# Three groups of steps at other places in a hand-written order: head 0's scores and weighing, two sets of shift products, the inverse's last step

## The chip, the core and the metric

The kernel runs on one core of a Trainium2 chip. Its engines each work through their own queue in the order in which the program issues to them: PE (TensorE, matmuls and transposes), DVE (VectorE), ACT (ScalarE), POOL (GpSimd, some additions and the feed of one weight stream) and SP (SyncE, the main weight stream). They meet only at semaphores. The metric is the device time of one launch in microseconds (us).

## The reference, cut to what matters

512 tokens of width 1024 go through a differential attention layer, then through a feed-forward layer, a mixer (pooling and a gated delta rule in chunks of 64) and a second feed-forward layer, each of the last three behind an RMS norm that is scaled and shifted by a conditioning vector. Everything is float32. Cut to the three places that the change touches:

```
# attention, 16 heads: two score maps a head, softmax each, weighed difference
a = softmax(q1 @ k1.T / 8 - slope * distance) - lam * softmax(q2 @ k2.T / 8 - slope * distance)
o = (1 - 0.2) * rms_norm(a @ v) * g

# each sublayer of the second block
h = rms_norm(x, norm_g) * (1 + scale) + shift          # then h @ w_in

# delta rule: one unit lower triangular system of 64 rows per head and chunk
sol = triangular_solve(a_mat + eye, rhs, lower=True, unit_diagonal=True)
```

## The kernel before, in words

`Plan` writes one list of steps by hand. Every engine walks the whole list and issues its own part of each step, in list order, so the place of a step in the list is its place in five queues at once. Nothing reorders them afterwards.

The unit of time in the list is one `mm` step: one 128x128 block of weights against 512 tokens, as three matmuls (lines 1202, 1203 and 1205) because the weights (`wH`, `wL`) and the activations (`hH`, `hL`) are kept as a high and a low part. The weights of 8 such blocks are a slot. SP loads a slot into `wr`, ACT writes its high part (line 1908, step `split`), DVE its low part (line 1497, same step). The `split` of slot j+3 stands behind the last block of slot j.

**Attention.** Iteration i of the loop over heads has 24 list positions, one behind each `mm` of the tiles q, k and v of head i (in iteration 1, q of head 1 has been done ahead, and positions 8 to 15 stand behind the blocks of k, 16 to 23 behind those of v). `SCHED` says at which position which small step of an earlier head stands; a position of 24 or more falls into the next iteration. Where several stand at one position, those from an earlier iteration come first, then `rstd`, `sq_lo`, `table`, `scores`, `weigh`, `turnw` and `ada`, in that order. For head 0 in iteration 1 `c0` and `w0` hold, for all others `c` and `w`.

- `scores` (query blocks of 128 rows): PE multiplies q by k (line 1266) into two of the banks 2, 3 and 4, DVE adds the distance term and takes the row maximum (line 1620, then line 1624), ACT exponentiates and sums (line 2007). Block 3 takes banks 3 and 4, and bank 4 is free when DVE has read block 2 in it.
- `weigh`: DVE alone, four dependent operations (lines 1630 to 1639), after the exponentials. It signals `w`.
- `turnw` (key block kb): PE transposes the weighed blocks kb to 3 (line 1278). For kb 0 the last transpose waits for `w` of block 3. The step of head 0 stands at position 4 of iteration 2.
- `rstd`: PE sums squares (line 1255), ACT takes Ln and Exp (lines 1996 and 1999), DVE scales q and k (line 1609). That of head 1 stands at position 1 of iteration 2.
- `ada`: PE products of the conditioning vector with weights that POOL feeds (line 1302).

**Shift products.** The first tiles behind a norm are multiplied by x before its norm is known. The shift's part of them is made apart: `shift_row` (lines 1543 and 1546, eight dependent DVE operations on a slot still in `wr`), and later `shift_sum` on PE (line 1219). Norm 1 has three such rows, during the output tiles of attention (16 blocks a tile, steps (c, k) = tile and block); norm 2 has two, during the output tiles of the first feed-forward layer (22 blocks a tile).

**Inverse.** `inverse(g, step)` for g 0 and 1 makes the five steps t, p5, y5, p6, y6, three ticks apart (a tick is one `mm` or one `pool_out` block). y6 (line 1426) multiplies on PE, and ACT and DVE copy its two banks back (lines 2156 and 1847).

Of the kernel before, what the change touches and what calls it, by code (L numbers as in the profile page):

```python
# [46 lines left out]
def shape_constants():  # L47
# [18 lines left out]
    for g, w in enumerate((2, 4, 8, 16)):  # L66
# [3 lines left out]
    return c  # L70

SCHED = {"rstd": 1, "v": 10, "table": 2, "c": [(9, (0, 1)), (14, (2,)), (18, (3,))], "w": [11, 12, 16, 21],
         "c0": [(14, (0, 1)), (17, (2,)), (20, (3,))], "w0": [16, 17, 19, 22], "d": [4, 7, 7, 13], "pv": 18, "ada": 30,
         "o": 5, "lo": (12, 18)}


# [34 lines left out]
def src(name, col, nk=8, row=0, cols=128):  # L111
    return (name, row, nk, col, cols)
# [19 lines left out]
class Plan:  # L132
# [13 lines left out]
    def sig(self, name):  # L146
        self.count[name] = self.count.get(name, 0) + 1
        return self.count[name]
# [4 lines left out]
    def add(self, what, **d):  # L153
        self.steps.append((what, d))
        return d
# [338 lines left out]
    def out0(self):  # L494
        sig, add = self.sig, self.add
        add("fold0", rn=self.count["rn"])
        z_free = [("gl", 0)] * 4
        zr = Ring(range(4))
        for h in range(6, HEADS):
            i, _ = zr.take()  # L500
            d = dict(h=h, i=i, free=z_free[i], zs=sig("zs"), zm=sig("zm"), gh=sig("gh"), gl=sig("gl"), on=self.on[h])
            z_free[i] = ("gl", d["gl"])
            self.whole(Tile("z", src("l0_w_in", 6144 + 128 * h), self.pb01.take()[1], "h", ("zs", d["zs"]), n=0, d=d))
            if h < 12:
                add("fold", h=h - 6, ze=h - 5, gh=sig("gh"), gl=sig("gl"))
        self.h_lasts[1] = len(self.slots)
        self.move("x_back", zm=self.count["zm"])
        self.move("mod_in")
        add("mod_wait")
        sq_free = [("gl", self.count["gl"])] * 4  # L510
        self.square_ring = zr

        def square(c):
            i, _ = zr.take()
            z_free[i] = self.square(1, c, v=("zb", i), free=z_free[i], acc_free=("gl", self.count["gl"]))

        first = len(self.slots) + 16
        more = {4: [lambda: add("mod_rest"), lambda: self.raw(1, 0), lambda: self.raw(1, 1)],
                5: [lambda c=c: self.raw(1, c) for c in (2, 3, 4)], 6: [lambda: self.raw(1, 5)], 7: [lambda: self.raw(1, 6)]}
        at = {(6, 9): lambda: self.shift_row(1, 0, first), (7, 1): lambda: self.shift_row(1, 1, first + 1),  # L520
              (7, 8): lambda: self.shift_row(1, 2, first + 2)}
        for c in range(8):
            r = sig("xr")
            t = Tile("res0", src("l0_w_out", 128 * c, 16), self.pb01.take()[1], "g", ("xr", r), c=c, xr=r)
            for k in self.steps_of(t):
                if k == 5 and c > 0:
                    square(c - 1)
                    for fn in more.get(c, []):
                        fn()
                if (c, k) in at:  # L530
                    at[c, k]()
            if c == 3:
                add("mod", modt=sig("modt"))
        self.last_square = lambda: square(7)

    def ffn(self, sub, w_in, w_out):
        sig, add = self.sig, self.add
        n = {0: 1, 2: 3}[sub]
        f = sub // 2
        add("ffn", f=f, n=n)  # L540
        pb = Ring(range(6))

        def gate(j, rhs="h"):
            fg = sig("fg")
            if rhs == "h":
                return Tile("gate", src(w_in, 128 * j), pb.take()[1], "h", ("fg", fg), n=n, j=j, f=f, fg=fg)
            gr = sig("gr")
            return Tile("gate", src(w_in, 128 * j), pb.take()[1], "r", ("gr", gr), n=n, j=j, f=f, fg=fg, gr=gr)

        def up(j, rhs="h"):  # L550
            d = dict(fu=sig("fu"), ah=sig("ah"), al=sig("al"))
            return Tile("up", src(w_in, FFN + 128 * j), pb.take()[1], rhs, ("fu", d["fu"]), n=n, j=j, f=f, fg=22 * f + j + 1,
                        **d)

        self.raw_start(n, gate(0, "r"), up(0, "r"), gate(1, "r"))
        self.whole(up(1))
        for j in range(2, 22):
            self.whole(gate(j))
            self.whole(up(j))
        self.h_lasts[n + 1] = len(self.slots)  # L560
        ring, s_free = Ring(range(2)), [("rs", 0)] * 2

        def square(c):
            i, _ = ring.take()
            s_free[i] = self.square(n + 1, c, v=("sq", f, i), free=s_free[i], acc_free=("nl", 8 * n + 8))

        first = len(self.slots) + 24
        for c in range(8):
            r = sig("xr")
            t = Tile("res", src(w_out, 128 * c, 22), pb.take()[1], "a", ("xr", r), c=c, xr=r, sub=sub, f=f, back=None)  # L570
            for k in self.steps_of(t):
                if k == 5 and c > 0:
                    square(c - 1)
                    if n == 1:
                        self.raw(2, c - 1)
                if n == 1 and c == 7 and k in (2, 9):
                    self.shift_row(2, k // 9, first + k // 9)
        self.last_square = lambda: square(7)
        if n == 3:
            square(7)  # L580

    def mixer(self):
        sig, add = self.sig, self.add
        n = 2
# [54 lines left out]
        def at(tick, fn, *a):  # L639

            n_ev[0] += 1
            events.append((tick, n_ev[0], fn, a))
# [138 lines left out]
        at(227, lambda: add("sol_back"))  # L781
        for g in range(2):
            for j, step in enumerate(("t", "p5", "y5", "p6", "y6")):
                at(251 + 16 * g + 3 * j, inverse, g, step)
        po = iter(range(8))
        for which in "kq":
            for g in range(2):
# [30 lines left out]
        for t in range(4):  # L818
            if t > 0:
                for g in range(2):  # L820
                    d = dict(g=g, t=t, ks=sig("ks"), rr=[sig("rr") for _ in range(4)], ur=ur[g], st=st[g])
# [14 lines left out]
            for g in range(2):  # L836
                om[g] = sig("om")
                d = dict(g=g, t=t, at=ro.take()[1], om=om[g], vv=vv[g], hq=sig("hq"), hn=sig("hn"), i=(2 * t + g) % 4)
# [37 lines left out]
        first = len(self.slots) + 8  # L876
# [1473 lines left out]
```

## Time and profile before

| | |
|---|---|
| median of 3 runs | 1902.35 us (1902.47, 1902.35, 1899.78) |
| profiled execution, its own time | 1900.43 us |
| its span, first to last instruction | 1898.6 us |
| mean granted TensorE clock | 0.997 |
| PE busy | 1869.9 us (98%) |
| DVE busy | 995.5 us (52%) |
| ACT busy | 818.2 us (43%) |
| POOL busy | 124.0 us (7%) |

Times inside a profile count from the start of its span. The profiled execution's own time is 1.83 us above the span, which is what lies ahead of the first and behind the last instruction. A row of a timeline gives the start, the length, the engine, the line and the operation, and in brackets how long the engine sat idle before it and what released it.

### The profile page before, as it was taken

To read this page: it belongs to the slowest core of one execution; us is meant where nothing else is said; L and a number is where in the kernel's file an instruction comes from. 1 tells how busy PE (TensorE), PEld (TensorE's weight loads), DVE (VectorE), ACT (ScalarE), POOL (GpSimd) and SP (SyncE) were. 2 spreads that over 40 slices of the span, in tenths; PEclk is the share of its full clock that TensorE was granted. 3 is DMA by queue.
4 is the path that set the end of the run, shared out by engine and by line. 5 is a ranking of instruction groups with operands and counts; after the bars stand their busy time and mean duration, and the time that the engine had idled before them with its cause. 6 is when DMAs were issued, how large, how long until landed. Compare 5 with 4: busy or idle time off the path is not lost.

```text
span 1898.6 us, 22387 instructions
## 1 busy us (share of the span) xinstructions
PE 1869.9 (98%) x8923; PEld 1448.7 (76%) x8923; DVE 995.5 (52%) x1778; ACT 818.2 (43%) x1328; POOL 124.0 (7%) x148
## 2 busy tenths in 40 slices
PE   8999999999999999999999999999999999999997
PEld 6566666666788788888886777778888878888886
DVE  6667666665544653333346667845434763333322
ACT  6566656656643342222324655434432442222221
POOL 0101111110001000000010011000000100000000
PEclk9999999999999999999999999999999999999999
DMA  5534333332233132222323313221123323222221
GB/s 199 182 127 162 137 144 145 146 143 101 78 132 114 67 111 100 95 95 93 100 87 124 104 65 106 70 92 35 45 89 111 124 90 103 94 100 97 92 93 62
DMA packets 56526, 201.95 MB, mean 106 GB/s; under 512 B 6478, under 2 KB 6934, under 8 KB 55784
## 3 DMA queue, kind: packets, MB, share of 16 engines
q1 hardware_dynamic: 44616, 158.32, 23.7%
q0 software_dynamic: 11808, 42.21, 6.1%
q8 instruction: 71, 1.16, 0.2%
q14 instruction: 31, 0.25, 0.0%
HBM read 195.23 MB, written 5.28 MB: 106 GB/s over the span
## 4 chain that ended last, share of the span: by engine, by line
PE 84%; DVE 8%; ACT 6%; issue 2%; DMA 0%; SPq 0%; DVEq 0%; ACTq 0%
PE ps L1202 24%; PE ps L1205 23%; PE ps L1203 23%; ACT wH L1908 2%; PE ps L1302 2%; PE ps L1338 1%; DVE a L1620 1%; DVE wL L1497 1%; PE ps L1266 1%; ACT a L2007 1%; PE ps L1290 1%; PE ps L1278 1%; PE ps L1345 1%; DVE g1a L1497 1%; PE ps L1255 1%
## 5 line engine op out<-in xcount | busy, mean ns | idle before, releaser
L1202 PE MATMUL ps<-hH,wH 128*128 128x512 f32 (+1 forms) x1560 | 635.7, 408 | 1.0 <-DVE hL L1568 1.0
L1205 PE MATMUL ps<-hH,wL 128*128 128x512 f32 (+1 forms) x1560 | 610.3, 391 | 1.0 <-DVE wL L1497 0.7
L1203 PE MATMUL ps<-hL,wH 128*128 128x512 f32 (+1 forms) x1560 | 608.7, 390 | 0.0
L1497 DVE TENSOR_TENSOR wL<-wr,wH 128x1024 fp32r<-128x1024 f32 (+2 forms) x285 | 343.9, 1207 | 490.8 <-ACT wH L1908 490.2
L1908 ACT ACTIVATE wH<-wr 128x1024 fp32r<-128x1024 f32 (+2 forms) x285 | 295.2, 1036 | 234.3 <-PE ps L1205 220.4
L1202 PEld LDWEIGHTS ps<-hH,wH 128*128 128x128 f32 (+1 forms) x1560 | 292.5, 187 | 97.0 <-issue 36.2
L1205 PEld LDWEIGHTS ps<-hH,wL 128*128 128x128 f32 (+1 forms) x1560 | 292.3, 187 | 67.5 <-DVE wL L1497 3.9
L1203 PEld LDWEIGHTS ps<-hL,wH 128*128 128x128 f32 (+1 forms) x1560 | 292.9, 188 | 60.7 <-issue 6.5
L1202 PE MATMUL ps<-gffn,wH 128*128 128x512 f32 x400 | 156.9, 392 | 1.0 <-DVE xT L1675 0.8
L1205 PE MATMUL ps<-gffn,wL 128*128 128x512 f32 x400 | 155.7, 389 | 0.0
L1203 PE MATMUL ps<-gffn,wH 128*128 128x512 f32 x400 | 155.6, 389 | 0.0
L2007 ACT ACTIVATE a<-a,tiny 128x128 f32<-128x128 f32 (+3 forms) x128 | 71.0, 555 | 154.3 <-DVE tiny L1624 154.3
L1908 ACT ACTIVATE gffn<-affn 128x512 fp32r<-128x512 f32 x44 | 27.8, 632 | 184.2 <-DVE affn L1697 181.0
L1202 PE MATMUL ps<-g,wH 128*128 128x512 f32 x224 | 89.1, 398 | 0.0
L1202 PEld LDWEIGHTS ps<-gffn,wH 128*128 128x128 f32 x400 | 75.1, 188 | 17.7 <-DVE xT L1675 1.3
L1203 PE MATMUL ps<-g,wH 128*128 128x512 f32 x224 | 87.4, 390 | 0.0
L1205 PE MATMUL ps<-g,wL 128*128 128x512 f32 x224 | 87.2, 389 | 0.0
L1203 PEld LDWEIGHTS ps<-gffn,wH 128*128 128x128 f32 x400 | 75.1, 188 | 15.8 <-issue 0.5
L1205 PEld LDWEIGHTS ps<-gffn,wL 128*128 128x128 f32 x400 | 75.1, 188 | 15.8
L1697 DVE TENSOR_TENSOR affn<-ps,affn 128x512 f32<-128x512 f32 x42 | 29.0, 691 | 101.9 <-PE ps L1205 100.1
L2062 ACT ACTIVATE affn<-ps 128x512 f32<-128x512 f32 x40 | 23.9, 597 | 117.0 <-PE ps L1205 117.0
L2234 POOL TENSOR_TENSOR affn<-affn 128x512 f32<-128x512 f32 x12 | 18.5, 1545 | 693.6 <-ACT affn L1934 693.6
(304 smaller groups left out, 2079.4 us busy)
## 6 DMA issues: line engine op xcount, KB each, us to landing
wr<-wst SPq DMA_DIRECT2D x268, 512.0 KB, 3.4
a<-wfd POOLq DMA_DIRECT2D x54, 512.0 KB, 4.8
xT<-wfd POOLq DMA_DIRECT2D x18, 512.0 KB, 6.8
wr<-wst SPq DMA_DIRECT2D x16, 384.0 KB, 2.9
xT<-xin SPq DMA_DIRECT2D x8, 256.0 KB, 7.5
xT<-xin SPq DMA_DIRECT2D x2, 1024.0 KB, 6.3
xsave<-xT SPq DMA_DIRECT2D x1, 2048.0 KB, 7.3
c<-wfd POOLq DMA_DIRECT2D x8, 256.0 KB, 3.4
```

Source lines behind the costliest of these rows:

```text
L1202: e.matmul(o, hi, xh[k], start=k == 0, stop=False)
L1203: e.matmul(o, hi, xl[k], start=False, stop=False)
L1205: i = e.matmul(o, lo, xh[k], start=False, stop=k == t.nk - 1)
L1255: e.matmul(b[:], m, sq_hi[j], start=True, stop=False)
L1266: i = e.matmul(ps[d["banks"][m]][:, a["at"]:a["at"] + n], qn[h % 2][64 * m:64 * m + 64, 128 * qb:128 * qb + 128], kn[h % 2][64 * m:64 * m ...
L1278: i = e.transpose(b4(b, qb - kb), Wr[h % 2][:, a:a + 128], C("ident"))
L1302: i = e.matmul(ps[7][32 * j:32 * j + 1, :], csil[:, k:k + 1], ada_buf[a % ADA_BUFS][:, 512 * (j % 2):512 * (j % 2) + 512], start=k == 0, s ...
L1497: e.tensor_tensor(dst, x, hi.bitcast(F32), ALU.subtract).then_inc(s[name], 1)
L1697: e.tensor_tensor(v, ps[t.bank][:], f["sg"][j % 2], ALU.mult).then_inc(s["fu"], 1)
L1908: e.activation(dst, x, ACT.Copy).then_inc(s[name], 1)
L2007: e.activation(v, v, ACT.Exp, bias=mx[:, m:m + 1], accum_out=rsum[:, m:m + 1]).then_inc(s["ex"], 1)
L2062: e.activation(v, ps[t.bank][:], ACT.Silu).then_inc(s["fg"], 1)
```

## The change

`scores` of head 0 go from positions 14, 17 and 20 (blocks 0 and 1, block 2, block 3) to 14, 20 and 23. Its `weigh` steps go from 16, 17, 19 and 22 to 17, 18, 22 and 26, and 26 is position 2 of iteration 2. The three shift rows of norm 1 go from (6, 9), (7, 1), (7, 8) to (5, 11), (6, 3), (6, 11), the two of norm 2 from (7, 2), (7, 9) to (6, 12), (7, 2). The y6 steps stand two ticks later, for g 0 and g 1. No instruction is added, taken away or altered in size.

```
-         "c0": [(14, (0, 1)), (17, (2,)), (20, (3,))], "w0": [16, 17, 19, 22], "d": [4, 7, 7, 13], "pv": 18, "ada": 30,
+         "c0": [(14, (0, 1)), (20, (2,)), (23, (3,))], "w0": [17, 18, 22, 26], "d": [4, 7, 7, 13], "pv": 18, "ada": 30,
...
-        at = {(6, 9): lambda: self.shift_row(1, 0, first), (7, 1): lambda: self.shift_row(1, 1, first + 1),
-              (7, 8): lambda: self.shift_row(1, 2, first + 2)}
+        at = {(5, 11): lambda: self.shift_row(1, 0, first), (6, 3): lambda: self.shift_row(1, 1, first + 1),
+              (6, 11): lambda: self.shift_row(1, 2, first + 2)}
...
-                if n == 1 and c == 7 and k in (2, 9):
-                    self.shift_row(2, k // 9, first + k // 9)
+                if n == 1 and (c, k) in ((6, 12), (7, 2)):
+                    self.shift_row(2, c - 6, first + c - 6)
...
-                at(251 + 16 * g + 3 * j, inverse, g, step)
+                at(251 + 16 * g + 3 * j + j // 4 * 2, inverse, g, step)
```

## Rows read from the trace of the kernel before

**Rows 1.** The profile's page, part 1: busy time of each engine.

```profile
PE 1869.9 (98%) x8923; PEld 1448.7 (76%) x8923; DVE 995.5 (52%) x1778; ACT 818.2 (43%) x1328; POOL 124.0 (7%) x148
```

**Rows 2.** Who PE waited for: us in total, times, longest.

```profile
PE ps L1266 <- DVE tiny L1620: 2.3, 1, 2.3
...
PE ps L1402 <- DVE a L1836: 1.5, 1, 1.5
```

**Rows 3.** Timeline of PE around head 0's scores: start, length, engine, line, idle before.

```profile
58.08 1.13 PE L1266 MATMUL ps<-a 64*128 64x512 f32 x4 [2.32 <-DVE tiny L1620]
...
67.72 0.60 PE L1278 MATMUL ps<-cst,a 128*128 128x128 f32 x4
68.07 0.48 PE L1202 MATMUL ps<-hH,wH 128*128 128x512 f32 x1
...
68.85 0.40 PE L1202 MATMUL ps<-hH,wH 128*128 128x512 f32 x1
...
69.54 0.39 PE L1202 MATMUL ps<-hH,wH 128*128 128x512 f32 x1
```

**Rows 4.** Timeline of DVE in the same stretch.

```profile
57.37 0.56 DVE L1620 CUSTOM_DVE_ANT_0 a<-ps,a 128x384 f32<-128x384 f32 x1
...
58.53 0.16 DVE L1630 RECIPROCAL tiny<-tiny 128x2 f32<-128x2 f32 x1
...
59.76 0.69 DVE L1497 TENSOR_TENSOR g1a<-a,g1a 128x512 fp32r<-128x512 f32 x1
60.36 0.16 DVE L1630 RECIPROCAL tiny<-tiny 128x2 f32<-128x2 f32 x1
...
61.80 0.69 DVE L1620 CUSTOM_DVE_ANT_0 a<-ps,a 128x512 f32<-128x512 f32 x1
...
64.90 0.17 DVE L1630 RECIPROCAL tiny<-tiny 128x2 f32<-128x2 f32 x1 [1.59 <-ACT a L2007]
...
66.54 0.69 DVE L1584 COPY xT<-ps 128x512 f32<-128x512 f32 x1
...
68.28 0.74 DVE L1609 SCALAR_TENSOR_TENSOR a<-a,tiny,xT 128x512 f32<-128x512 f32 x1
```

**Rows 5.** Timeline of ACT in the same stretch.

```profile
58.65 0.61 ACT L2007 ACTIVATE a<-a,tiny 128x384 f32<-128x384 f32 x1 [3.68 <-DVE tiny L1624]
...
59.77 0.19 ACT L2007 ACTIVATION_READ_ACCUMULATOR a<-a,tiny 128x1 f32 x1
63.34 0.72 ACT L2007 ACTIVATE a<-a,tiny 128x512 f32<-128x512 f32 x1 [3.38 <-DVE tiny L1624]
...
65.72 1.24 ACT L1996 ACTIVATE xT<-ps,cst 128x512 f32<-128x512 f32 x2
66.86 1.15 ACT L1999 ACTIVATE xT<-xT 128x512 f32<-128x512 f32 x2
```

**Rows 6.** A window: length; PE, PEld, DVE, ACT, POOL busy; granted clock; DMA.

```profile
1289.58:1292.99 3.41, 3.41 (x14) 2.37 (x13) 0.69 (x1) 0.69 (x2) 0.00 (x0) 0.50 0.02 5
```

**Rows 7.** Timeline of PE and DVE at the end of attention's output tiles.

```profile
641.24 2.68 DVE L1546 SCALAR_TENSOR_TENSOR b<-wr,tiny,b 128x128 f32<-128x128 f32 x7
...
643.34 0.39 PE L1205 MATMUL ps<-g,wL 128*128 128x512 f32 x1
...
643.83 0.69 DVE L1675 TENSOR_TENSOR xT<-ps,xT 128x512 f32<-128x512 f32 x1
```

**Rows 8.** The page, part 6: DMA issues, KB each, us to landing.

```profile
wr<-wst SPq DMA_DIRECT2D x268, 512.0 KB, 3.4
```

**Rows 9.** Timeline of DVE at the end of the first feed-forward layer.

```profile
1005.05 1.23 DVE L1497 TENSOR_TENSOR wL<-wr,wH 128x1024 fp32r<-128x1024 f32 x1 [1.30 <-ACT wH L1908]
```

**Rows 10.** Timeline of PE and ACT around y6 of g 0.

```profile
1273.88 2.08 PE L1426 MATMUL ps<-a 64*64 64x64 f32 x32
1275.06 0.59 ACT L2156 ACTIVATE a<-ps 64x512 f32<-64x512 f32 x1 [1.17 <-PE ps L1426]
...
1278.75 1.91 PE L1381 MATMUL ps<-cst,a 128*128 128x128 f32 x16
```

## The prediction

> **What bounds the kernel now.** The page comes first: PE is busy for 98% of the span, the next engine for 52% [rows 1]. No PE instruction is added or taken away, so all that the change can do is to open or close gaps in PE's work. The list of what PE waited for comes next. Of its waits two lie at steps that the change touches or stands beside: 2.3 us in one piece at line 1266, head 0's scores, and 1.5 us at line 1402, y5 of the inverse [rows 2]. So the most that the attention part can win is 2.3 us, 0.12% of the time, less than what a measurement of this kernel can tell from no change (0.2%, 3.8 us). What it can lose has no such limit, so I follow each queue around the new places.
>
> **Why PE waits at head 0's scores now.** PE reaches `scores` of block 3 at 58.08 - 2.32 = 55.76 and starts at 58.08 [rows 3]. It needs bank 4, in which block 2 stands until DVE has taken its maximum, and DVE starts on that at 57.37 [rows 4]: 0.71 from the start of DVE's instruction to PE. DVE was late for that, not PE.
>
> **The attention part, step by step.** The new order on DVE behind the `split` and `weigh` of block 0, which it finishes at 57.37 as before, since what is ahead of them stays, is: `sq_lo` of head 1's k, `weigh` 1, maxima of block 2, `weigh` 2, the copy of v, a `split`, maxima of block 3, `rstd` of head 1, `weigh` 3. The lengths are start to start from [rows 4]: block 2's maxima 58.53 - 57.37 = 1.16; `weigh` 1 59.76 - 58.53 = 1.23; `sq_lo` 0.60; `weigh` 2 61.80 - 60.36 = 1.44; `weigh` 3 66.54 - 64.90 = 1.64; copy and `split` together 68.28 - 66.54 = 1.74. Block 3's maxima start at 61.80 and ACT starts its exponentials at 63.34 [rows 4, 5]: 1.54, of which 1.34 is DVE's up to its last small operation.
>
> - DVE starts block 2's maxima at 57.37 + 0.60 + 1.23 = 59.20, ready at 60.36.
> - PE reaches `scores` of block 3 three `mm` steps later than before. A step is 69.54 - 68.85 = 0.69 [rows 3], so 55.76 + 2.07 = 57.83. It can start at 59.20 + 0.71 = 59.91. The wait of 2.32 becomes one of 2.08. That is all the gain, 0.24: two more pieces of DVE work now stand ahead of block 2, and PE is given about as much time as they take.
> - ACT exponentiates block 2 in 59.77 + 0.19 - 58.65 = 1.31, begun 0.12 after DVE is through (58.65 against 58.53) [rows 4, 5]: 60.48 to 61.79. `weigh` 2 waits for it (before, it was ready): 61.80 to 63.24. Copy and `split` to 64.98.
> - Block 3's maxima 64.98, exponentials from 66.52, done 64.90 - 63.34 = 1.56 later [rows 4, 5]: 68.08.
> - ACT only then turns to `rstd` of head 1: two Ln in 66.86 - 65.72 = 1.14, then the first Exp, half of 1.15 plus about 0.1 to reach DVE [rows 5]: 68.08 + 1.14 + 0.66 = 69.88. Its PE sums are long there: by PE's order they are done before `ada`, so well ahead of the 67.48 below.
> - DVE scales q and k of head 1, two operations of 0.74 that overlap to about 1.35 [rows 4]: 71.2. `weigh` 3 takes 1.64 and ends at about 72.85. Before it ended at 66.54, because it stood ahead of the copy, the `split` and `rstd`.
>
> PE gets to `turnw` of kb 0 at 67.72 in the kernel before, and goes on with the next `mm` at 68.07 [rows 3]. Now it gets there at 67.72 - 0.24 = 67.48. Three of its transposes can run; the fourth waits for `weigh` 3, and the next `mm` starts at about 73.1. **This part therefore costs 73.1 - 68.07 = 5.0 us**, as one stop of about 5.3 us less the 0.24. Everything behind the stopped transpose on PE waits with it: the remaining blocks of head 2's q, hence its `out_qk` on ACT and the next `split`. These hang on PE, so they arrive late by the same 5.0 and are not late against it. Nothing later takes it back, since PE is the busy engine and none of its later waits hangs on a clock of its own. POOL's `table` for head 1 waits for block 3's maxima (by the sum above 66.5 instead of 63.3), and the maxima of head 1, which read it, come more than 10 us later; the feed of `ada` behind it has the same cover. SP has no step that moves.
>
> The bounds of this part: if `rstd` came through on ACT before block 3 (it stands behind it in the list, so this needs my order to be wrong), the stop would be shorter by 1.8 + 1.35, about 2 us left. If DVE loses time where I overlap, up to 1 us more. Taken: 5.0, between 2 and 6.
>
> **The clock.** The stop has a second price that no instruction shows. The granted clock was 0.50 for 3.41 us from 1289.58 [rows 6], that is 1.2 instead of 2.4 GHz. It fell after PE had waited 1.5 us [rows 2] and then done narrow 32-row products, an estimate of 2.5 us with little work in all. It didn't fall after the 2.32 us at 58.08. A stop of 5.3 us is twice either. One stretch at half clock costs at most 3.41 / 2 = 1.7 us. I take 1.6, and 0 to 3.4 (none, or two stretches) as bounds. The Trainium skill, "TensorE: Matmul & The Clock Gate", section "HAM oscillation — how this bites in real kernels", says that a wait between bursts of matmuls sets PE back to half its clock and that the rise is paid again each time; it speaks against this change, and without it the sum would be 1.6 us lower. The trace agrees in kind with its 0.50 from 1289.58.
>
> **Shift rows of norm 1.** Each row is one operation and seven of 2.68 us together, some 3.0 us of DVE [rows 7]. The last one ended on 643.83, when DVE took up the sum for x; PE's last product there began at 643.34 and was over at 643.73 [rows 7]. So DVE was late by 0.1 us or less, and only that is won: 0.06. The rows go to a tile earlier, where DVE has the same room, behind the `split` of the same stretch, and the slot that each reads is there: SP asks for it once the `split` four slots earlier is done, which stands 12 `mm` steps ahead, 8.3 us, and a slot lands in 3.4 us [rows 8]. If it were late, DVE would wait, and behind it on DVE a `split` that PE needs some 9 us later: still 0. POOL adds squares beside the second one, which slows DVE there by about a microsecond, hidden by the same cover. Without that cover it would cost its 1 us.
>
> **Shift rows of norm 2.** DVE was waiting for ACT again, 1.30 us, before the last tile's last `split` [rows 9], so the old rows held nobody up. 0, between -0.1 and +0.3.
>
> **y6 two ticks later.** y6 of g 0 starts at 1273.88, ACT copies at 1275.06, and the next step that takes one of its banks starts at 1278.75 [rows 10]. Two `mm` steps are 1.4 us, so the copy ends at about 1277.0: still early. PE waited for neither y6, so nothing is won. The wait at y5 is DVE's copy behind a conv step, which stays. 0, between -0.3 and +0.3; without the gap of 3 us it would cost up to the 1.4.
>
> **The sum.** 5.0 + 1.6 - 0.06 = +6.6 us. Against the profiled execution's own 1900.43 that is 1907.0. The median of the runs shown is 1.9 higher, 1902.35, and would give 1908.9. The four executions at hand lie at 1899.78, 1900.43, 1902.35 and 1902.47, and I take their middle, 1901.4: **1908.0 us**.
>
> **The rivals.**
>
> - *The stop costs no clock, and the stretch at half clock at 1289.58 goes.* That one hangs on a short stop of 1.5 us, so a small shift might spare it; for it speaks that a similar stop at 58.08 cost no clock. Against it: the new stop is much longer. 5.0 - 1.6 = 3.4, on 1901.4: 1904.8, within 0.2% of before. 0.20.
> - *No new wait (other side: faster).* The place is the fourth transpose at 67.48. If `weigh` 3 is done by then, nothing is lost, and if the wait at the scores goes too, 2.3 is won: 1899.1. For it: DVE is busy for 52% only, so there is room. Against it: the chain from block 2's maxima on is dependent work on two engines, and needs 5.3 us less than its own rows give. It decides only where that chain shortens by all of 5.3. 0.04.
> - *The clock stays low for longer* or falls at both stops, 57.83 and 67.5: 5.0 + 3.4 and the stretch at 1289.58 kept: 1909.8, and with DVE's lost microsecond 1911. 0.12.
>
> **How the numbers follow.** The forecast has 0.64, with a range of its own from 1905.5 to 1911.0: 1901.4 or 1902.35 as base, 4 to 6 for the stop, 0 to 3.4 for the clock. The range for all is 1903.5 to 1911.5. It takes in the first rival and most of the last, and leaves out the one on the other side and the tails. Slower by over 0.2% (above 1906.15) are the forecast and the last rival less their low ends: 0.73. Within 0.2%: the first rival and those ends: 0.22. Faster: 0.05.
>
> **What would show it.** In the profile after: PE waiting about 5 us at line 1278 for DVE line 1639 near 67.5, a wait of about 2 us still at line 1266 near 57.8, `rstd` on DVE (line 1609) ahead of the last `weigh`, a stretch with granted clock 0.50 right behind, and all later steps some 5 to 7 us later. The waits at the two norms and at the inverse should stand as they were. I am wrong if the wait at line 1278 is under 3 us, or if the later waits at line 1202 or 1402 shrink by more than a microsecond.

## The result, and the profile after

| | before | changed |
|---|---|---|
| median (lowest to highest) | 1902.22 us (1899.78 to 1903.31), 11 runs | 1906.24 us (1905.73 to 1907.98), 11 runs |
| profiled execution, its own time | 1900.43 us | 1906.26 us |
| its span | 1898.6 us | 1904.5 us |

The ratio is 1.0026, 95% interval [1.0018, 1.0034]: slower by 4.0 us. The forecast was 1908.0, range 1903.5 to 1911.5, and slower.

The list of what PE waited for in the changed kernel, beside [rows 2]:

```profile
PE ps L1278 <- DVE a L1639: 3.3, 1, 3.3
...
PE ps L1266 <- DVE tiny L1620: 1.9, 1, 1.9
...
PE ps L1402 <- DVE a L1836: 1.5, 1, 1.5
...
PE ps L1202 <- DVE xT L1675: 0.8, 1, 0.8
```

There is one new line, DVE line 1639 (the last operation of a weighing), and the wait at the scores has fallen from 2.3 to 1.9 us. The waits at y5 and at norm 1 stand as before.

Timeline of PE in the changed kernel, answering to [rows 3]:

```profile
59.96 1.13 PE L1266 MATMUL ps<-a 64*128 64x512 f32 x4 [1.87 <-DVE tiny L1620]
...
61.98 0.63 PE L1202 MATMUL ps<-hH,wH 128*128 128x512 f32 x1
...
69.11 0.49 PE L1278 MATMUL ps<-cst,a 128*128 128x128 f32 x3
72.90 0.47 PE L1278 MATMUL ps<-cst,a 128*128 128x128 f32 x1 [3.30 <-DVE a L1639]
73.03 0.77 PE L1202 MATMUL ps<-hH,wH 128*128 128x512 f32 x1
```

Three transposes of head 0 run at 69.11, the fourth at 72.90, and the next `mm` starts at 73.03. The matmul at 61.98 is 0.63 us long where the same kind took 0.39: half clock.

DVE in the changed kernel, answering to [rows 4]:

```profile
57.42 0.68 DVE L1497 TENSOR_TENSOR g1a<-a,g1a 128x512 fp32r<-128x512 f32 x1
...
59.25 0.55 DVE L1620 CUSTOM_DVE_ANT_0 a<-ps,a 128x384 f32<-128x384 f32 x1
...
61.86 0.17 DVE L1630 RECIPROCAL tiny<-tiny 128x2 f32<-128x2 f32 x1 [1.37 <-ACT a L2007]
...
63.31 0.68 DVE L1584 COPY xT<-ps 128x512 f32<-128x512 f32 x1
...
65.04 0.69 DVE L1620 CUSTOM_DVE_ANT_0 a<-ps,a 128x512 f32<-128x512 f32 x1
...
69.80 0.75 DVE L1609 SCALAR_TENSOR_TENSOR a<-a,tiny,xT 128x512 f32<-128x512 f32 x1 [3.25 <-ACT xT L1999]
...
71.13 0.16 DVE L1630 RECIPROCAL tiny<-tiny 128x2 f32<-128x2 f32 x1
...
72.09 0.75 DVE L1639 SCALAR_TENSOR_TENSOR a<-a,tiny 128x512 f32<-128x512 f32 x1
```

And ACT, answering to [rows 5]:

```profile
60.52 0.61 ACT L2007 ACTIVATE a<-a,tiny 128x384 f32<-128x384 f32 x1 [5.38 <-DVE tiny L1624]
...
66.58 0.72 ACT L2007 ACTIVATE a<-a,tiny 128x512 f32<-128x512 f32 x1 [3.80 <-DVE tiny L1624]
...
68.01 1.24 ACT L1996 ACTIVATE xT<-ps,cst 128x512 f32<-128x512 f32 x2
69.15 1.14 ACT L1999 ACTIVATE xT<-xT 128x512 f32<-128x512 f32 x2
```

Read the two together. At 61.86 DVE takes up `weigh` 2, which had to wait for ACT; at 65.04 the maxima of block 3, behind copy and `split`; at 69.80 q of head 1, 3.25 us idle before it because ACT takes the Ln of line 1996 only after block 3's exponentials; at 71.13 the last weighing, whose last operation starts at 72.09. PE goes on 0.06 us after its end.

Windows of the changed kernel (columns as in [rows 6]):

```profile
61.61:65.02 3.41, 3.41 (x10) 2.64 (x9) 3.05 (x6) 1.17 (x3) 0.00 (x0) 0.50 0.00 0
69.60:72.90 3.30, 0.00 (x0) 0.00 (x0) 2.94 (x6) 0.69 (x2) 1.25 (x3) 0.84 0.84 268
72.90:78.40 5.50, 5.50 (x16) 4.52 (x17) 0.00 (x0) 1.71 (x3) 0.00 (x0) 0.50 0.54 220
1288.00:1300.00 12.00, 10.50 (x215) 8.40 (x215) 5.85 (x8) 4.40 (x7) 0.00 (x0) 1.00 0.15 46
```

The granted clock is 0.50 for 3.41 us behind the wait at the scores, and again for 6.83 us from 71.85 on, of which 1.05 still lie within the stop at the transposes. Near 1290 us, where [rows 6] had a stretch at 0.50, it is 1.00.

Timeline around y6 of g 0 in the changed kernel, answering to [rows 10]:

```profile
1282.59 2.08 PE L1426 MATMUL ps<-a 64*64 64x64 f32 x32
1283.77 0.59 ACT L2156 ACTIVATE a<-ps 64x512 f32<-64x512 f32 x1 [2.55 <-PE ps L1426]
...
1286.09 1.91 PE L1381 MATMUL ps<-cst,a 128*128 128x128 f32 x16
```

y6 stands 1.4 us nearer to the next step that needs its bank (3.50 us from start to start, 4.87 before), as worked out, and its copy still ends ahead of it. The last sum for x at norm 1 [rows 7] holds PE for 0.8 us as before, in the list above.

### The profile page after: what moved, and what is told of

Read it like the earlier page. It is cut to its first block, busy times and chain, and to the rows that moved or that the text cites. A ratio compares the mean times of both kernels' runs of the same rounds, so it can differ in the third digit from the quotient of the medians.

```text
span 1904.5 us, 22387 instructions
## 1 busy us (share of the span) xinstructions
PE 1873.5 (98%) x8923; PEld 1451.5 (76%) x8923; DVE 995.6 (52%) x1778; ACT 818.3 (43%) x1328; POOL 124.7 (7%) x148
## 4 chain that ended last, share of the span: by engine, by line
PE 85%; DVE 7%; ACT 5%; issue 2%; DMA 0%; SPq 0%; DVEq 0%; ACTq 0%
PE ps L1202 24%; PE ps L1205 24%; PE ps L1203 24%; PE ps L1302 2%; ACT wH L1908 2%; PE ps L1338 1%; DVE a L1620 1%; PE ps L1266 1%; DVE wL L1497 1%; ACT a L2007 1%; PE ps L1290 1%; PE ps L1278 1%; PE ps L1345 1%; PE ps L1255 1%; DVE g1a L1497 1%
```

## The experiments

Each kernel was timed beside the kernel before on the same chip. The median of the kernel before lay there at 1902.08 us (for attention part only, rows and y6 only, last weighing at 24, only last weighing moved), at 1901.39 (block 3 at 22, the two with a stop filled, before again) and at 1901.82 (y5 later, block 3 at 22 and y5 later, changed again). Three distances are compared besides the time. The first two begin at the first `scores` matmul of head 0 (line 1266, at 45.71 in the profile before): one ends at the `mm` behind head 0's first transposes, the other at head 0's `pv` (line 1290, at 82.19 in the profile before). The third is what is left from there to the end of the span. They leave out what lies ahead of the first `scores`, where nothing was changed and which still ends anywhere from 44.49 us (attention part only) to 46.58 us (block 3 at 22) in the thirteen profiles. At that beginning a matmul of line 1203 at 11.24 us already takes 0.39 us in the one, and one at 13.13 still 0.63 in the other, so half clock at the start of the launch, of differing length, is part of it; PE's waits for constants and for ACT there differ as well. The half-clock column lists where the granted clock was 0.50, for 3.41 us unless noted; the stretch at the very end of each launch, when PE has nothing left to do, isn't listed.

| kernel | median, us | ratio to before [95%] | to the `mm` | to `pv` | `pv` to the end | half clock at |
|---|---|---|---|---|---|---|
| before | 1902.22 | | 22.36 | 36.48 | 1816.4 | 1289.6 |
| before again | 1900.48 | 0.9997 [0.9988, 1.0006] | 22.32 | 36.43 | 1816.5 | 1288.6 |
| changed | 1906.24 | 1.0026 [1.0018, 1.0034] | 27.12 | 43.84 | 1814.7 | 61.6; 71.9 (6.83 us) |
| changed again | 1905.61 | 1.0023 [1.0014, 1.0032] | 27.12 | 43.77 | 1814.6 | 61.1; 71.4 (6.83 us) |
| attention part only | 1906.09 | 1.0024 [1.0016, 1.0033] | 27.10 | 42.81 | 1816.7 | 58.6; 72.2; 1294.2 |
| rows and y6 only | 1901.74 | 0.9999 [0.9991, 1.0008] | 23.94 | 38.04 | 1816.5 | 58.3; 1290.5 |
| last weighing at 24 | 1901.61 | 1.0003 [0.9994, 1.0011] | 24.11 | 38.24 | 1816.5 | 1290.8 |
| only last weighing moved | 1901.88 | 1.0006 [0.9997, 1.0014] | 25.49 | 39.65 | 1815.0 | 57.0 (6.83 us) |
| block 3 at 22 | 1897.52 | 0.9980 [0.9971, 0.9989] | 21.12 | 35.23 | 1816.5 | 1288.6 |
| changed, stop filled | 1904.78 | 1.0019 [1.0010, 1.0028] | 28.61 | 42.72 | 1814.8 | 60.9 |
| before, stop filled | 1898.85 | 0.9990 [0.9981, 0.9999] | 22.19 | 36.31 | 1814.8 | none |
| y5 later | 1897.13 | 0.9982 [0.9973, 0.9991] | 23.78 | 37.89 | 1813.4 | 57.2 |
| block 3 at 22 and y5 later | 1895.15 | 0.9969 [0.9956, 0.9981] | 21.11 | 35.23 | 1813.5 | none |

The last two columns go together. Of the eleven profiles with y5 at its old place, the six with a stretch near 1290 take 1816.4 to 1816.7 us from `pv` to the end, the five without it 1814.6 to 1815.0: that stretch costs 1.6 us or a little more.

### The attention part alone

```
-"c0": [(14, (0, 1)), (17, (2,)), (20, (3,))], "w0": [16, 17, 19, 22]
+"c0": [(14, (0, 1)), (20, (2,)), (23, (3,))], "w0": [17, 18, 22, 26]
```

Expected: 

> Only the attention part of the change (head 0's scores at 14, 20, 23, its weighing at 17, 18, 22, 26), shift rows and y6 as before. Theory 1 (all of the loss is in this part): the same as the changed kernel, 4.0 us over the kernel before, and the same waits, about 1.9 us at line 1266 and a stop at line 1278 that ends when DVE's line 1639 is done at about 72.9. Theory 2 (the moved shift rows or y6 cost or win something): at least 1 us away from the changed kernel.

Measured: 1906.09 us, 0.15 from the changed kernel, with its two waits (whom PE waited for, us, times, longest):

```profile
PE ps L1278 <- DVE a L1639: 3.5, 2, 3.3
...
PE ps L1266 <- DVE tiny L1620: 2.0, 1, 2.0
```

Theory 1 holds: all of the loss is in this part. Two of its 12 executions, however, lie at 1902.7 and 1902.9 us, the others from 1904.9 to 1907.5, while none of the 21 of the changed kernel is under 1904.7; why these two are faster wasn't seen.

### Shift rows and y6 alone

The other hunks of the change, with `c0` and `w0` as before.

Expected: 

> Only the other two parts: shift rows of both norms and y6 at their new places, attention as before. Theory 1: no difference, within 1 us, with 0.06 us won where DVE takes up x at the last output tile of attention. Theory 2: 1 us or more, either way. The clock can still differ by a stretch at half clock of 3.4 us, worth up to 1.7 us, since the new steps stand near 1289 us where one lay in the profiled execution of before.

Measured: ratio 0.9999 [0.9991, 1.0008], an interval that reaches 1.7 us down and 1.5 up. The profile is sharper: from head 0's `pv` to the end, where all the moved rows and y6 steps lie, it takes 1816.5 us against 1816.4, both with the stretch near 1290. Theory 2 falls, and the 0.06 us of theory 1 is too small to be seen. Its windows show something else:

```profile
58.28:61.69 3.41, 3.41 (x9) 1.61 (x6) 3.16 (x13) 1.30 (x4) 0.00 (x0) 0.50 0.58 225
1290.49:1293.90 3.41, 3.41 (x9) 2.36 (x8) 1.25 (x2) 0.47 (x1) 0.00 (x0) 0.50 0.02 5
```

The attention part here is that of the kernel before, and yet 3.41 us at 0.50 stand behind the wait at the scores, which the profiled execution of before did not have. The way to the `mm` is 1.6 us longer for it (23.94 against 22.36). So the kernel before has this stretch too, in some executions.

### The last weighing ahead of rstd

```
-"w0": [17, 18, 22, 26]
+"w0": [17, 18, 22, 24]
```

Expected: 

> Attention part as in the change, but the last weighing at 24, position 0 of iteration 2, ahead of head 1's rstd in place of behind it. Theory 1: DVE takes it up when block 3's exponentials are done at about 68.1, ends at about 69.8, and PE goes on at about 70.0, 3.1 us earlier than in the changed kernel; over the kernel before about 1.9 us, plus or minus what the clock does. Rival (the stop hangs on the exponentials of block 3, not on where the weighing stands): no gain over the attention part alone, PE goes on at about 73.

DVE and PE in that kernel:

```profile
68.25 0.17 DVE L1630 RECIPROCAL tiny<-tiny 128x2 f32<-128x2 f32 x1 [1.59 <-ACT a L2007]
...
68.84 0.55 PE L1278 MATMUL ps<-cst,a 128*128 128x128 f32 x3 [1.02 <-ACT xT L1996]
...
69.92 0.75 DVE L1609 SCALAR_TENSOR_TENSOR a<-a,tiny,xT 128x512 f32<-128x512 f32 x1
...
70.03 0.33 PE L1278 MATMUL ps<-cst,a 128*128 128x128 f32 x1 [0.64 <-DVE a L1639]
...
70.11 0.48 PE L1202 MATMUL ps<-hH,wH 128*128 128x512 f32 x1
```

The weighing now begins at 68.25, right behind the exponentials, and `rstd` (69.92) comes behind it. PE goes on with the `mm` at 70.11, 3.0 us nearer to the first scores than in the changed kernel (24.11 against 27.12) and 1.75 further than before: the 1.9 expected. The rival falls, as place and not readiness set the stop. But the median, 1901.61, isn't 1.9 over before; the ratio is 1.0003. Here I had missed something in the total, not in the stretch.

### Only the last weighing moved

```
-"w0": [16, 17, 19, 22]
+"w0": [16, 17, 19, 26]
```

Expected: 

> Everything as before but the last weighing of head 0, which goes from 22 to 26, behind head 1's rstd. Theory 1: DVE does copy and split while ACT exponentiates, then waits for Exp of rstd, scales q and k until about 69.3 and ends the weighing at about 70.6; PE stops at line 1278 from 67.8 to 70.7 and loses 2.6 us. The wait of 2.3 us at line 1266 stays. Rival: no stop, since the weighing's inputs are ready at 64.9 as before.

```profile
67.55 0.75 DVE L1609 SCALAR_TENSOR_TENSOR a<-a,tiny,xT 128x512 f32<-128x512 f32 x1 [0.96 <-ACT xT L1999]
...
68.88 0.16 DVE L1630 RECIPROCAL tiny<-tiny 128x2 f32<-128x2 f32 x1
...
70.08 0.90 PE L1278 MATMUL ps<-cst,a 128*128 128x128 f32 x4
...
70.73 0.47 PE L1202 MATMUL ps<-hH,wH 128*128 128x512 f32 x1
```

```profile
56.98:63.81 6.83, 6.21 (x14) 3.87 (x15) 5.56 (x19) 2.26 (x7) 1.10 (x1) 0.50 0.40 155
1280.00:1300.00 20.00, 18.50 (x284) 15.29 (x282) 10.26 (x14) 7.50 (x12) 0.00 (x0) 1.00 0.17 55
```

The first listing is DVE and PE around the transposes, the second has the windows of its half-clock stretch and of the inverse. The weighing (68.88) is behind q and k (67.55) as expected, and the way to the `mm` is 25.49, 3.1 longer than before. PE however barely waits: it comes to the transposes at 70.08, late by itself, because the clock was 0.50 for 6.83 us from 56.98 on, within and behind the wait at the scores. The time that PE lost there would otherwise have been spent waiting at the transposes. The median is that of before (0.2 us under it, 1.1 over it by the ratio), where 2.6 over it was expected. That the stretch's price hides in the stop explains part of it, and in this profile the stretch near 1290 is missing as well. How much each makes in the median isn't settled by one profile.

### Block 3 two steps later, its weighing where it was

```
-"c0": [(14, (0, 1)), (17, (2,)), (20, (3,))]
+"c0": [(14, (0, 1)), (17, (2,)), (22, (3,))]
```

Expected: 

> A version meant to win: only block 3's scores of head 0 go from 20 to 22, its weighing stays at 22 behind it. DVE's and ACT's orders stay the same, and on PE two mm steps stand ahead of the scores in place of behind them. Theory: the wait at line 1266 shrinks from 2.3 to about 0.9 us, PE reaches head 0's transposes 1.4 us earlier, at 66.3, and waits there about 0.3 us for the weighing that ends at 66.6; 1.1 us faster than before, less than can be told from no change, but the waits of the profile show it. A stretch at half clock may go with the shorter stop (1.7 us at most). Rival: PE's wait at the scores stays at 2.3.

```profile
PE ps L1266 <- DVE tiny L1620: 0.9, 1, 0.9
```

The wait is 0.9, as worked out, and the way to `pv` is 1.25 us shorter. The median is 3.9 us lower than that of before (3.8 by the ratio), three times as much: a gain that the waits don't explain. Eight of the 11 executions lie from 1896.1 to 1897.7 us, the other three, the profiled one among them, from 1899.6 to 1900.5.

### The stops filled

In the changed kernel, ahead of the fourth transpose:

```
+if h == 0 and kb == 0 and qb == 3:
+    w.wait_ge(s["am"], 6)
+    for _ in range(22):
+        e.matmul(ps[2][:], wH[:, 0:128], hH[:, 0:512], start=True, stop=True)
 w.wait_ge(s["w"], 4 * h + qb + 1)
```

Expected: 

> The changed kernel with 22 extra matmuls of 512 columns (their results are not used, into a bank that is free) ahead of the fourth transpose of head 0, where PE stops. At full clock they take 5.0 us, so they are over at about 74.2 at the earliest if started at 69.2, 1.2 us later than the stop ended. If the clock is what costs more than the stop: the stretch at half clock behind the stop goes, 2.5 us are won there and 1.2 lost, so about 1.3 us faster than the changed kernel. If the clock costs nothing, 1.2 us or more slower than the changed kernel.

```profile
68.86 5.27 PE L1280 MATMUL ps<-hH,wH 128*128 128x512 f32 x22
73.97 0.27 PE L1282 MATMUL ps<-cst,a 128*128 128x128 f32 x1
73.99 0.47 PE L1202 MATMUL ps<-hH,wH 128*128 128x512 f32 x1
74.31 0.39 PE L1203 MATMUL ps<-hL,wH 128*128 128x512 f32 x1
```

The fill runs from 68.86 over 5.27 us and PE goes on at 73.99, 28.61 behind the first scores: 1.5 us later than in the changed kernel. And the matmuls behind it take 0.40 in place of 0.63. To `pv` it is 42.72 against 43.84, so 1.1 us have been won back by then: 2.6 us of clock behind the stop. In the traces it is so 1.1 us faster than the changed kernel, with 22 matmuls more, and the clock behind the stop was worth 2.6 us there. The times say the same but don't show it by themselves: the ratios to before, 1.0019 against 1.0026 and 1.0023 for the changed kernel, are 1.3 and 0.8 us apart, and their intervals overlap.

In the kernel before, ahead of block 3's scores:

```
+for _ in range(9):
+    e.matmul(ps[d["banks"][0]][:], wH[:, 2048:2176], hH[:, 0:512], start=True, stop=True)
```

Expected: 

> The kernel before with 9 extra matmuls of 512 columns (results not used) into bank 3 ahead of block 3's scores of head 0, where PE waits 2.3 us. They take about 2.05 us, so PE's wait falls to 0.3 us and the scores start when they did. If most executions of the kernel before lose clock at this stop (the profiled one, 1900.43, did not, and the median is 1.8 us over it): about 1.7 us faster than before. If not: no difference.

```profile
55.85 2.20 PE L1263 MATMUL ps<-hH,wH 128*128 128x512 f32 x9
58.12 1.13 PE L1269 MATMUL ps<-a 64*128 64x512 f32 x4
```

The scores start when they did (58.12 against 58.08) and the way to `pv` is as before, 36.31. But the median falls by 2.5 us (1.9 by the ratio), and how it falls can be seen in the single executions. Of all 110 timed executions of the kernel before, 36 lie from 1897.6 to 1899.8 us and 74 from 1900.8 to 1903.3, with nothing between. (The profiled execution, 1900.43, is not among them and belongs to neither.) With the stop filled, all 11 lie from 1898.4 to 1899.6: the upper group is gone. Nine idle-time matmuls take it away, so that group is the executions in which the wait at the scores has a price beyond its length. That the price is the clock is borne out by the mean granted clock, which is on record for 99 of the 110. It is 0.996 or 0.997 in all 64 of the upper group, and 0.998 or 0.999 in 29 of the 35 of the lower (0.997 in the other six); with the stop filled it is 0.998 or 0.999 in ten of 11. One stretch of 3.41 us at 0.50 lowers this mean by 0.001. Where in the launch the upper group's clock was lost the means don't say; in the profile of the rows and y6 alone it is behind the wait at the scores.

### Before once more, changed once more

Unaltered kernels, for second profiles.

Expected: 

> The kernel before, unchanged, for a second profile: 1.000 to itself. If the stretches at half clock fall differently from execution to execution, this profile has them at other places or in other number than the first (one, from 1289.58), with the same waits on semaphores to 0.3 us, and its time differs by up to 1.7 us for each.

Measured: the waits on DVE as before, the profile again one of the lower group (1288.6 its only stretch). The expectation's "other places or number" was not met by this pair; only the profile of the rows and y6 alone, whose steps around the scores are those of before, has another stretch. The median, 1900.48, lies between the two groups, five executions in each.

Expected: 

> The changed kernel once more, for a second profile and for its distance to the kernel before on this chip: 4 us over it. Theory (the stops set the clock back in each execution, only how many stretches differ): again at least one stretch at half clock between 58 and 80 us, and the same waits at lines 1266 and 1278 by their ends, whatever their shares of stop and slow work are.

Measured: 27.12 to the `mm` and 43.77 to `pv`, stretches at the same two places, 3.8 us over before by medians. Met.

### The inverse's y5 later

```
-at(251 + 16 * g + 3 * j, inverse, g, step)
+at(251 + 16 * g + 3 * j + (2 if g and j >= 2 else 0), inverse, g, step)
```

Expected: 

> The kernel before with y5, p6 and y6 of the inverse's g 1 two ticks later (t and p5 stay): two mm steps of 1.4 us stand between p5 and y5 more than before. Theory: the wait of 1.5 us at y5 (line 1402, near 1287 us) falls to about 0.1, and the stretch at half clock behind it, worth 1.6 us, goes; 1.5 to 3.1 us faster than before. Rival: the copy that y5 waits for stands behind a conv step that is late by the same amount, so the wait stays: no difference.

All that PE still waited for from 1200 to 1400 us:

```profile
PE ps L1434 <- ACT o L2136: 0.3, 1, 0.3
```

The wait at line 1402 is gone, and so is the stretch near 1290. The median is 1897.13, 4.7 us under before; the ratio gives 3.4 (0.9982 [0.9973, 0.9991]). In the profile it is 3.0 us from `pv` to the end, 1813.4 against 1816.4. The theory is met, with a size at or somewhat above its upper end, 3.1; the rival falls. The profile has a stretch behind the scores that the one of before had not, so its own span is only 2.2 us shorter.

Both together:

Expected: 

> Both: block 3's scores of head 0 at 22, and y5, p6, y6 of g 1 two ticks later. If the two gains add up: 3.9 us (measured for the first alone) plus 1.5 to 3.1, so 5.4 to 7 us faster than before, about 1895.5. If they share the clock's part, about 4.5 us.

```profile
44.00:84.00 40.00, 38.48 (x187) 23.38 (x186) 24.65 (x74) 22.75 (x51) 5.71 (x9) 1.00 0.56 208
1280.00:1300.00 20.00, 19.86 (x279) 15.53 (x278) 11.30 (x16) 7.24 (x12) 0.00 (x0) 1.00 0.18 55
```

1895.15 us of 5 executions, ratio 0.9969 [0.9956, 0.9981], 6.7 us under the kernel before by medians and 5.9 by the ratio. In the profile the gains add up to 0.1 us: 35.23 to `pv` as in block 3 at 22, 1813.5 from there as in y5 later. In the time they are within the 5.4 to 7 expected, but below the sum of the two single gains (3.8 and 3.4 by the ratios), and the interval, 3.6 to 8.4 us, doesn't exclude that a part is shared. The listing has the windows around head 0 and around the inverse, both at full clock. This version beats both kernels.

## Why the prediction was right, and where it was off

- *The whole effect is in the attention part; shift rows and y6 at nothing.* Right. They gave 0.9999 alone, `pv` to the end took 1816.5 us against 1816.4, and the wait at norm 1 (line 1675) is still 0.8.
- *The wait at the scores stays.* Right: 2.08 forecast, 1.87 measured. DVE began on block 2 at 59.25 (59.20 forecast).
- *DVE's and ACT's chain.* Right to about 0.1 at each link: block 3's maxima 65.04 (64.98), its exponentials 66.58 (66.52), q of head 1 69.80 (69.88), PE on with the `mm` at 73.03 (73.1). So 5.0 us, as one sum, came out as 4.8 by the distance (27.12 less 22.36).
- *"One stop of about 5.3 us."* The place was right, the size wasn't: 3.30. PE came to the transposes at 69.11 and not 67.48, since half clock behind the first wait slowed it by 1.6 on the way; the rest of the difference is the three transposes that it could do. The end of the stop hangs on DVE, so that loss cost nothing more. The sign of being wrong that the prediction names, under 3 us at line 1278, was missed by only 0.3.
- *The clock's term of 1.6.* This is the step that was mis-sized. Behind the stop the clock cost 2.6 in the profile of the changed kernel (43.84 less 27.12 is 16.72, and 36.48 less 22.36 is 14.12) and 2.5 in its second one. With the attention part alone, whose stretch there is 3.41 us and not 6.83, it was 1.6 (42.81 less 27.10 is 15.71), the size that I took. But I added such a term to the changed kernel only. The kernel before pays for its own wait at the scores in 74 of 110 executions; filling that wait gave 2.5 us by medians. And the stretch near 1290 us, in both profiles of before, is absent from both profiles of the changed kernel, 1.7 the other way (1816.4 against 1814.7). 4.8 + 2.6 - 2.5 = 4.9, and with the 1.7 taken off too 3.2; the measured 4.0 lies between. The profile with the stop filled has no stretch near 1290 either, so its 2.5 may hold some of the 1.7 already. For the profiled pair, where before had no stretch at the scores, it is 7.4 to `pv`, less 1.7, and 0.2 from the beginning: 5.9, the difference of the spans. And beside the kernel before with its stop filled, the one profile of these with no stretch at all, everything closes: 43.84 - 36.31 = 7.5, the spans are 7.5 apart (1904.5 and 1897.0), the medians 7.4.
- *The effect and the base.* The forecast effect was 6.6 and the measured one 4.0. The stop took 4.8 of the 5.0 given to it, so what was off is the clock's net part: +1.6 forecast, 4.0 - 4.8 = -0.8 measured, because before pays as well and the stretch near 1290 went. The forecast time was nearer than that, 1.8 over the measured one, by luck: I took as base the middle, 1901.4, of four executions that come from unlike states of the clock, and it lay 0.8 under the median of 1902.22. The middle of two groups describes neither.
- *The rivals.* The first, no clock price and the later stretch gone, is half true: the stretch went, the price was paid. It gave 1904.8, 1.4 from the measured 1906.24, where the forecast's 1908.0 is 1.8 from it. The one of no new wait is out by the 3.30 us at line 1278. The one of the clock falling at both stops happened, in all three profiles of the changed attention part with nothing filled in (changed, changed again, attention part only), but its first stretch was hidden in the second stop, so its price of 3.4 was too high.

What stays open: these sums are made of single profiles and medians, each good to half a microsecond or so. The two groups of the kernel before are about 3 us apart, while the stretch behind the scores costs 1.6 and 1.4 in the two profiles that have it with the old attention part (23.94 and 23.78 against 22.36). The stretch near 1290 (1.7) and the beginning (up to 2.1) can make up the rest, but which executions have which was not seen. Why a stretch comes in one execution and not in another isn't known either, and the length of the wait doesn't decide it. At the scores, waits of 1.8 to 2.7 us have one in seven profiles, waits of 2.1 to 2.3 have none in three (before, before again, last weighing at 24). Near 1290, the wait is 1.5 us in all eleven profiles with the old y5, and six of them have the stretch. And the medians of "last weighing at 24" and "only last weighing moved" equal that of before, although the way to `pv` is 1.8 and 3.2 us longer than in before's profile. That they lose less clock, or hide it in the stop, fits their profiles and, for the first, the mean granted clock, which is 0.998 in seven of its 11 executions and 0.997 in four. But its executions spread from 1899.8 to 1903.2 us at that clock, which nothing here explains.

## What to carry to other kernels

Moving a step in a shared order moves it in all queues. Cost it as a chain of single instructions, start to start, through each engine that it touches, and look for the last reader: giving a producer a later place (here the last weighing behind `rstd`) costs the consumer that kept its place. Where PE waits on a chain, the remedy is to put more PE work ahead of the wait and leave the producers' order alone: block 3 at 22 and y5 two ticks later did only that. And where PE is busy for 98%, its few short waits can cost more than their length, because of the clock behind them: here 1.4 and 1.5 us of wait removed gave 3.9 and 3.4 to 4.7 us. A change in one of them is then to be priced against a kernel before that may pay for its own waits, and a median of a few executions from two groups is no base.

## What the runs showed of the hardware that was not expected

- A wait of PE of about 2 us at the scores, or one of 1.5 us with 1.1 us of narrow products behind it, goes with 3.41 us or more at half clock in some profiles and not in others with the same steps there; at the scores the stretch can begin within the wait. The time of the kernel before falls into two groups some 3 us apart, the upper one at the lower mean clock, and 9 matmuls in that wait remove the upper one.
- Useless matmuls in a wait can make a kernel faster: 9 of them 2.5 us by the median, 22 of them 1.1 us in the trace, although they overran the wait by 1.5 us. The Trainium skill, "TensorE: Matmul & The Clock Gate", section "HAM oscillation — how this bites in real kernels", tells of kernels in which waits between bursts of matmuls set PE to half clock again and again; the trace agrees in kind, with 0.50 behind the waits in the profiles named above, and shows that a single wait can be enough.
- Half clock ahead of a stop whose end hangs on another engine was free here: the stretch from 61.61 in the changed kernel made PE 1.6 us later at the transposes and the stop as much shorter. Behind the stop, 5.78 us at half clock cost 2.6, somewhat under half their length.
